# Norm sums by output groups, a first chunk in row quarters, and one split moved, in a two-layer MLA / RG-LRU / MoE trunk

## What is computed

```python
DEPTH = 2; D_MODEL = 1024; T = 16 meta tokens + 256 tokens = 272
for l in range(DEPTH):
    u = rmsnorm(h, norm_mix_g[l])                  # norm 1
    cq, ckv, kr, xr, gt = split(u @ w_in[l])       # 384, 256, 32, 512, 512 columns
    att = mla_mixer(cq, ckv, kr, ...)              # 8 heads, QK-norm, rotary keys
    rnn = rglru_mixer(xr, gt, ...)                 # conv, gates, linear recurrence, gelu gate
    h = h + concat(rmsnorm(att), rmsnorm(rnn)) @ w_out[l]
    u = rmsnorm(h, norm_ffn_g[l])                  # norm 2
    h = h + (swiglu(u), 2816 wide | moe_swiglu(u), top 2 of 8 experts, 1408 wide)[l]
return h[:, N_META:]
```

## Time and profile before

| | us |
|---|---|
| median of three runs | 901.33 |
| the profiled execution | 902.6 |
| its span | 900.6 |
| TensorE busy in it | 868.4 (96%) |
| VectorE busy | 683.5 (76%) |
| ScalarE busy | 574.1 (64%) |
| chain that ended last, on TensorE | 81% |

### The profile page before, as it was taken

One profiled execution on the slowest core, in us unless ns is written; L12 is line 12 of the kernel. 1 busy time (PEld: TensorE's weight loads), 2 busy tenths in 40 slices (PEclk: granted clock), 3 DMA queues, 4 the chain that ended last, 5 costly groups with the idle time before them and its releaser, 6 DMA issues.

```text
span 900.6 us, 15424 instructions
## 1 busy us (share of the span) xinstructions
PE 868.4 (96%) x5825; PEld 798.1 (89%) x5825; DVE 683.5 (76%) x919; ACT 574.1 (64%) x787; POOL 69.5 (8%) x92
## 2 busy tenths in 40 slices
PE   5998999999999999999999999999999999999995
PEld 4965799999999999966899989999998989999994
DVE  5777877666666554787877889799897989789892
ACT  6476656455544443476746777877778777777772
POOL 4450010000000000000132000000000000000000
PEclk9999999999999999999999999999999999999998
DMA  9614025455478553414054899899998999899991
GB/s 299 202 48 142 2 95 187 142 186 179 160 208 236 150 170 112 141 48 140 8 211 170 295 355 373 307 350 400 338 396 300 375 370 364 315 361 380 356 350 27
DMA packets 120748, 208.18 MB, mean 231 GB/s; under 512 B 5872, under 2 KB 73712, under 8 KB 120688
## 3 DMA queue, kind: packets, MB, share of 16 engines
q1 hardware_dynamic: 118976, 201.94, 63.7%
q0 software_dynamic: 1424, 5.24, 2.9%
q10 hardware_dynamic: 288, 0.20, 0.1%
HBM read 202.12 MB, written 5.24 MB: 230 GB/s over the span
## 4 chain that ended last, share of the span: by engine, by line
PE 81%; DVE 10%; ACT 4%; issue 2%; POOL 2%; DMA 1%; SPq 0%; DVEq 0%; ACTq 0%; POOLq 0%
PE ps L2427 24%; PE ps L2452 13%; PE ps L637 11%; PE ps L639 11%; PE ps L638 11%; DVE wlo L1382 4%; PE ps L2392 2%; PE ps L2157 2%; PE ps L1964 1%; ACT whi L940 1%; PE ps L2207 1%; DMA raw<-in_w_in_dram 1%; PE ps L2041 1%; PE ps L2439 1%; PE ps L1969 1%
## 5 line engine op out<-in xcount | busy, mean ns | idle before, releaser
L1382 DVE TENSOR_TENSOR wlo<-raw,whi 128x1536 fp32r<-128x1536 f32 (+4 forms) x296 | 437.9, 1502 | 97.2 <-ACT whi L940 94.6
L940 ACT ACTIVATE whi<-raw 128x1536 fp32r<-128x1536 f32 (+4 forms) x296 | 375.8, 1283 | 159.9 <-PE ps L639 93.2
L637 PE MATMUL ps<-uhi,whi 128*128 128x272 f32 (+1 forms) x576 | 169.9, 295 | 11.6 <-DVE wlo L1382 10.4
L639 PE MATMUL ps<-uhi,wlo 128*128 128x272 f32 (+1 forms) x576 | 166.9, 290 | 0.0
L638 PE MATMUL ps<-ulo,whi 128*128 128x272 f32 (+1 forms) x576 | 166.4, 289 | 0.0
L2427 PE MATMUL ps<-whi,xeh 128*128 128x320 f32 (+1 forms) x512 | 125.7, 326 | 0.0
L2427 PE MATMUL ps<-wlo,xeh 128*128 128x320 f32 (+1 forms) x512 | 124.3, 324 | 0.0
L2427 PE MATMUL ps<-whi,xel 128*128 128x320 f32 (+1 forms) x512 | 124.3, 324 | 0.0
L637 PEld LDWEIGHTS ps<-uhi,whi 128*128 128x128 f32 (+1 forms) x576 | 108.8, 189 | 13.3 <-issue 11.2
L638 PEld LDWEIGHTS ps<-ulo,whi 128*128 128x128 f32 (+1 forms) x576 | 109.1, 189 | 0.5
L639 PEld LDWEIGHTS ps<-uhi,wlo 128*128 128x128 f32 (+1 forms) x576 | 108.8, 189 | 0.0
(11 more groups left out here) (298 smaller groups left out, 1212.6 us busy)
## 6 DMA issues: line engine op xcount, KB each, us to landing
raw<-in_moe_w_down_dram SPq DMA_DIRECT2D x24, 1536.0 KB, 8.9
raw<-in_moe_w_gate_dram SPq DMA_DIRECT2D x16, 1536.0 KB, 7.3
raw<-in_moe_w_up_dram SPq DMA_DIRECT2D x16, 1536.0 KB, 8.3
raw<-in_moe_w_gate_dram SPq DMA_DIRECT2D x16, 1280.0 KB, 9.3
raw<-in_moe_w_up_dram SPq DMA_DIRECT2D x16, 1280.0 KB, 9.1
raw<-in_ffn_w_gate_dram SPq DMA_DIRECT2D x11, 1024.0 KB, 5.2
raw<-in_ffn_w_up_dram SPq DMA_DIRECT2D x11, 1024.0 KB, 5.1
raw<-in_ffn_w_down_dram SPq DMA_DIRECT2D x8, 1408.0 KB, 6.8
```

The lines of the kernel that those rows point to most:

```text
L637: pe.matmul(dst, wh, xh, start=start, stop=False, skip_group_check=True)
L639: return pe.matmul(dst, wl, xh, start=False, stop=stop, skip_group_check=True)
L940: act.activation(placed(whi, s, src), src, ACT.Copy).then_inc(hi_done, 1)
L1382: dve.tensor_tensor(placed(wlo, s, src), src, placed(whi, s, src).bitcast(F32), ALU.subtract).then_inc(lo_done, 1)
```

## The change

1. `total` over 8 chunks becomes `total_by_groups`: chunk c goes to output partitions 32 (c mod 4) to 32 (c mod 4) + 31, with 32 columns of ones. ScalarE copies the bank to SBUF, and one matmul with 128 columns of ones adds up the 128 partitions (`total`), so that the scale is divided by 32 more. The groups' sum of norm 1 stands behind q2 and the last matmul behind kv0 (both layers); of norm 2 of layer 0, behind dense blocks 0 and 1.
2. The recurrent half's squares likewise: 4 matmuls of 32 columns, a copy to `tb` by VectorE, and one single-column matmul for each tile, one step later in the loop of `values`. On VectorE `averages(2)` moves ahead of `normed(0)` and `normed(1)`.
3. w_in's first chunk is split in four row quarters (two token chunks, all 384 columns), in both layers. The three q blocks are done quarter by quarter in three banks (18 matmuls a quarter). In layer 0 the loads are in quarters too, the tokens' first quarter on ScalarE's queue, and the constants and positions behind the second chunk of w_in. MIX_SPLIT becomes 23.
4. Pieces kv0, kv1 and kr are split before the root, and the others five blocks ahead by number.
5. Five fp32 matmuls on a constant tile at the start of TensorE's list (WARM).
6. In w_out, `out_turned(0)`, `out_turned(1)` and `scale_spread` move behind block 1, and `out_turned(2)` behind block 2.
7. The fourth dense piece (`ff(3)`) is split behind the last chunk of `hT` and no longer ahead of it.

```diff
-MIX_SPLIT = 22
+PARTS = 4
+MIX_SPLIT = 23
+WARM = 5
...
+            def later(k):
+                return [PARTS + 3] if k == 0 else [k + SPL + 1] if k >= QC else []
...
+                        for m in range(PARTS):
+                            v = slice(2 * m, 2 * m + 2)
+                            if m:
+                                sp.dma_start(hT[:, v, :], ins["tokens"][:, v, :]).then_inc(x_in[m], 16)
+                            sp.dma_start(slot_of(n, k, c)[:, v, :], src[:, v, :]) ...
...
+                    if not l and j == 1:
+                        sp.dma_start(con[:, :], ins["constants"]).then_inc(con_in, 16)
+                        sp.dma_start(posi[:, :], positions.to_broadcast([P, SEQ])).then_inc(pos_in, 16)
...
+            act.dma_start(hT[:, 0:2, :], ins["tokens"][:, 0:2, :]).then_inc(x_in[0], 16)
             act.dma_start(vec[:, :], ins["columns"]).then_inc(vec_in, 16)
-            act.dma_start(posi[:, :], positions.to_broadcast([P, SEQ])).then_inc(pos_in, 16)
...
+            for m in range(PARTS):
+                first_high(2 * m)
+                first_high(2 * m + 1)
+                mix(0, m)
+            first_squares(range(KD))
+            mix(0, PARTS, PARTS + 1, PARTS + 2)
...
-                    mix(l, 2, 3)
-                root_all(B[l, "n1ss"], rsb[:, :], D, n1_root)
+                    mix(l, 2, 3, PARTS, PARTS + 1, PARTS + 2)
+                take(B[l, "n1part"], rsb[:, :])
+                root_all(B[l, "n1ss"], rsb[:, :], ROPE * D, n1_root)
...
-                    mix(l, k + SPL)
+                    mix(l, *later(k))
...
-                    if m >= SPL and l == 0:
+                    if m >= SPL and l == 0 and m < KD - 1:
                         ff(m - SPL)
...
                 if l == 0:
+                    ff(KD - 1 - SPL)
                     mark(ACT.Sqrt)
                     act.wait_ge(n2_filled, 1)
+                    act.activation(rsb[:, :], ps[:, 4, 0:T], ACT.Copy).then_inc(n2_part, 1)
+                    act.wait_ge(n2_filled, 2)
...
+                group_sums()
+                turned(2, META)
+                rn_variance()
                 mix(l, N_IN + 2)
-                rn_variance()
-                turned(2, META)
+                averages(2)
                 if l == 0:
                     normed(0)
                 normed(1)
-                averages(2)
...
+            def total_by_groups(bk, src):
+                for c in range(KD):
+                    g = c % 4
+                    q = pe.matmul(ps[ROPE * g:ROPE * (g + 1), bk, 0:T], ones(slice(0, P), ROPE), src[:, c, :],
+                                  start=(c < 4), stop=(c >= 4), skip_group_check=True)
                 return q
+            def total(bk):
+                return pe.matmul(ps[:, bk, 0:T], ones(slice(0, P), P), rsb[:, :], start=True, stop=True)
...
+            for _ in range(WARM):
+                pe.matmul(ps[:, 7, 0:T], rr[:, 0:P], rr[:, :], start=True, stop=True)
...
+                def query_latents():
+                    for part in range(PARTS):
+                        s = SPLIT0[l] + part
+                        chunk_ready(s)
+                        for c in range(QC):
+                            b = B[l, "q", c]
+                            if part == 0:
+                                fill(pe, b)
+                            for k in range(2):
+                                kk = 2 * part + k
+                                if c == 0:
+                                    pe.wait_ge(ulo_done, 2 * KD * l + kk + 1)
+                                ...
+                                q = matmul3(pe, bank(b), w, normed_in(kk, slice(0, T)), kk == 0, kk == KD - 1)
...
+                def squares_by_groups():
+                    for c in range(CH):
+                        q = pe.matmul(ps[ROPE * c:ROPE * (c + 1), b.bank, c0:T], ones(slice(0, P), ROPE), ta[:, c, c0:T],
+                                      start=True, stop=True, skip_group_check=True)
...
-                        for c in range(CH):
-                            q = pe.matmul(ps[0:n, b.bank, t:t + 1], ta[:, c, lead:lead + n], one[:, :], start=(c == 0),
-                                          stop=(c == CH - 1))
+                        q = pe.matmul(ps[0:n, b.bank, t:t + 1], tb[:, 0, lead:lead + n], one[:, :], start=True, stop=True)
...
-                    if m == 0:
+                    if m == 1:
                         if l == 0:
                             out_turned(0)
                         out_turned(1)
                         scale_spread()
-                    if m == 1:
+                    if m == 2:
                         out_turned(2)
```

More of the change, by code:

```diff
@@ L461, in build @@
         emptied = [sem(f"emptied{b}") for b in range(8)]
-        x_in = [sem(f"x{n}_in") for n in range(2)]
-        first_in = [sem(f"first{n}_in") for n in range(2)]
+        x_in = [sem(f"x{n}_in") for n in range(PARTS)]
+        first_in = [sem(f"first{n}_in") for n in range(PARTS - 1)]
+        part_used = sem("part_used")
         con_in = sem("con_in")
@@ L929, in split @@
             def split(s, land, src, i=0, chunks=0):
-                if land == MIX0[0] and s < QC - 1:
+                if land == MIX0[0] and s < PARTS - 1:
                     act.wait_ge(first_in[s], 16)
@@ L938, in split @@
                 elif s >= SPL:
-                    act.wait_ge(filled, piece_used(s - SPL) + 2 * chunks * i)
+                    old = [(l, s - SPL - SPLIT0[l]) for l in range(DEPTH) if 0 <= s - SPL - SPLIT0[l] < PARTS - 1]
+                    if old:
+                        act.wait_ge(part_used, (PARTS - 1) * old[0][0] + old[0][1] + 1)
+                    else:
+                        act.wait_ge(filled, piece_used(s - SPL) + 2 * chunks * i)
                 act.activation(placed(whi, s, src), src, ACT.Copy).then_inc(hi_done, 1)
@@ L1701, in _ @@
                         mix(l, N_IN + SPL + m)
-                    elif l == 0:
+                    elif l == 0 and m < KD - 1:
                         ff(m - SPL)
@@ L1959, in sums @@
                 return q
-            def total(bk, src, n):
-                for c in range(n):
-                    q = pe.matmul(ps[:, bk, 0:T], ones(slice(0, P), P), src[:, c, :], start=(c == 0), stop=(c == n - 1))
-                return q
+            def total_by_groups(bk, src):
[3 more added lines that the diff above has]
+                                  start=(c < 4), stop=(c >= 4), skip_group_check=True)
+                return q
+            def total(bk):
+                return pe.matmul(ps[:, bk, 0:T], ones(slice(0, P), P), rsb[:, :], start=True, stop=True)
             def spread(bk, row, width=P):
@@ L2135, in gate_half @@
                         fill(pe, b)
-                    q = dense_block(b, SPLIT0[l] + k, ks, W_IN_PIECES[k][2], 0, normed_in, start=half == 0, stop=half == 1)
+                    q = dense_block(b, SPLIT0[l] + PARTS - QC + k, ks, W_IN_PIECES[k][2], 0, normed_in, start=half == 0, stop=half == 1)
                     if half:
@@ L2179, in values @@
                         if t == 2 and i == VAR_AT:
+                            squares_by_groups()
+                        if t == 2 and i == VAR_AT + 1:
                             variance()
@@ L2307, in group @@
                                 pe.wait_ge(nsq_done, 2 * KD)
-                                total(4, u32, KD).then_inc(n2_filled, 1)
+                                total_by_groups(4, u32).then_inc(n2_filled, 1)
+                            if not per and m == 1:
+                                pe.wait_ge(n2_part, 1)
+                                total(4).then_inc(n2_filled, 1)
                     group([0, 1, 2, 3], FFS0, 0, 0, [B["ff0", q].before for q in range(4)])
```

118 lines of the change are left out of this document (62 added, 56 removed).

## The result

The changed kernel takes 897.65 us (median of 20 runs, 894.47 to 901.96) where the kernel before takes 902.38 (20 runs, 900.82 to 907.41): a ratio of 0.9941, interval 0.9928 to 0.9953. By the ratio that is 5.3 us less (4.2 to 6.5), by the two medians alone 4.7. The forecast was 7.1 us less. The two profiled executions differ by more, 902.6 and 894.47 us (spans 900.6 and 892.5, 8.1 apart).

What follows compares the result with a forecast made beforehand. TensorE, busy 96% of the span, was taken as the bound; 4.5 (start) + 0.2 (layer 1's norm 1) + 2.4 (norm 2) + 0 (output projection) = 7.1 us off 901.33 gives 894.2, own range 892 to 897, 8 in 10 889.5 to 898.5.

Steps and rivals of the forecast that it cites:

- The start: Layer 0 to the latents' sum: first matmul at 8.6 us, TensorE waits 1.5 us at that sum, 4.5 us won.
- rival 2: Start: warm-ups end too soon or do not count, first 20 matmuls at 0.226, 2.1 us more, 896.3; chance 0.20.
- I take it as up: Start: TensorE's clock is already up after 4.6 us of warm-up matmuls, so matmuls take 0.125 us each.
- The norms: Layer 1's norm 1 wins 0.2 us; layer 0's norm 2 wins 2.4, 0.6 of it by the moved split.
- The drains of 0.3 us: Grouped sums: tiling-mode changes might drain TensorE twice each; at 0.3 us, three norms would lose 1.8, time 896.
- The recurrent squares and the transposes: Output projection, both layers: about 0.6 us won by grouping, spent in a 1 us wait at `mixlo`; 0 in all.
- What is left of 6.1 us is 4.6: Layer 0: kv1 begins 6.1 us sooner, a 1.5 us wait follows at the latents' sum, the rest reaches the end.
- the existing fall: TensorE's clock granted at 0.69 and 0.63 between 85 and 95 us; vanishing would widen the range by 2 to 3.
- Rival 3: Clock falls at four new TensorE waits, at most 3.0 us each; four give 906.2, slower than before; chance 0.04.
- last sign of being wrong: Anywhere in the kernel: the forecast is wrong if the clock falls in other places.

Runs made afterwards that it cites:

- e9: The changed kernel with the loads of the constants and positions ahead of the second weight chunk again: 896.81 us, ratio 0.9932.
- e10: The kernel of e7 with the loads of the constants and positions ahead of the second weight chunk: 891.93 us, ratio 0.9900.
- a0: The changed kernel itself run again, unedited, for a second profile: 899.5 us, ratio 0.9947.
- e1: The changed kernel without the five warm-up matmuls: 896.32 us, ratio 0.9935.
- e4: The changed kernel with ScalarE's squares of the latents taken as soon as their own blocks are scaled: 896.02 us, ratio 0.9929.
- e3: The changed kernel with the three norms' squares summed by eight full matmuls instead of four groups, single matmul kept: 904.25 us, ratio 1.0015.
- e8: The changed kernel with the split of the fourth dense piece ahead of the last low part again: 898.45 us, ratio 0.9952.
- e2: The changed kernel with the transposes of the attention's output back at their old places: 896.09 us, ratio 0.9935.
- e5: The changed kernel with the latents' root, xr0's convolution and the reciprocal ahead of the split of the first gate piece: 896.89 us, ratio 0.9932.
- b0: The kernel before the change run again, unedited, for a second profile: 902.41 us, ratio 0.9991.
- e6: The changed kernel with e4's and e5's orders together, and VectorE's convolution of xr1 behind its scaling of the latents: 891.62 us, ratio 0.9890.
- e7: The kernel of e6 with the transposes at their old places as in e2: 890.70 us, ratio 0.9869.

## Why the prediction was right, and where it was off

**The number.** 897.65 us lies inside the range of 8 in 10 (889.5 to 898.5), but 0.65 outside the forecast's own 892 to 897, and 3.4 above the 894.2 predicted. Of that, 1.05 is the starting point: the sum was taken off a median of three runs (901.33), and twenty runs of the same kernel gave 902.38. The other 2.4 is the gain: 4.7 by medians where 7.1 was forecast.

**The start: right in time, luckier than argued.** Forecast 4.5 us at the latents' sum, measured 4.39; the first matmul at 8.04, not 8.6. TensorE's wait there was to be 1.5 us and is 2.31: TensorE ended xr0 0.5 us sooner than in the sum (31.03), and VectorE's chain from the reciprocal to the scaled kr, begun 0.6 sooner, took 8.9 us and not 8.2, because three of its splits were 0.1 to 0.3 us longer each, beside POOL's work on the angles. The earlier start paid for that. The Trainium skill, GPSIMD Engine Reference, 1. Specifications, says that GpSimd shares its SBUF interface with VectorE, with contention where a VectorE instruction has two SBUF inputs; the trace agrees: the splits (raw and whi) stretch, while the scalings, which read one operand from PSUM, stay at 0.44. In e9, where POOL's work ends 4.9 us sooner (29.3 us), all three splits take 1.22; but not every split beside POOL is longer (the one at 31.81 took 1.23), and in e10 two of the three stretch again. So this cause is likely, and not shown.

**The warm-ups: rival 2 is a matter of the execution.** Of eleven profiled executions with warm-ups, nine start at full pace and two (a0, e9) run at 0.226 to about 12.0 us, although the warm-ups lie at 2.57 to 7.47 us in both a0 and the first profile. The price is 1.8 us at the grouped sum (19.01 and 17.25), where rival 2 had 2.1. Without them (e1) the grouped sum comes at 18.45, so in these single executions warm-ups that work win 1.2 us and warm-ups that fail lose 0.6. The prediction's "I take it as up" was right in nine of eleven, with less margin than it seemed: in the nine, the first clock record of the trace, a rise to full, lies between 5.88 and 8.04 us, in one of them (e4) only as the first product begins.

**The norms: right.** Norm 2 and layer 1's norm 1 were to win 2.6 and won 2.61 (layer 1's own stage, from q0's first matmul to the latents' sum, 24.55 and 24.78 before: 0.2, as forecast); a grouped sum has the 1.15 us that the earlier trace rows gave, e3 puts 2.5 on each, e8 0.54 on the moved split. The drains of 0.3 us that the prediction weighed against it do not show: from the grouped sum's first matmul to the next block it is 1.06 us (17.25 to 18.31), and the steps into it and behind it (17.04 to 17.25, 18.31 to 18.54) are each 0.1 us longer than the pace.

**The recurrent squares and the transposes: right.** Forecast 0 with a wait of 1 us at `mixlo`; measured waits 0.97 and 1.06, stages -0.10 and -0.27. e2 shows both halves.

**The step that failed: "What is left of 6.1 us is 4.6", passed on to the end.** I followed VectorE as far as the latents' sum, in both layers, and let everything behind it come earlier by the same amount. In layer 1 it did not: 1.22 us were lost between that sum and the scores, and 0.18 in layer 0, where another loss was won back (there the kernel before waited 0.82 us for VectorE in the head norms' stage, and that wait is gone):

```profile
70.62 1.55 PE L2101 MATMUL ps<-raw,ckv 128*128 128x512 f32 x3 [0.82 <-DVE ksq L1491]
```

The cause, shown by e5: the whole chain ran closer to the transfer of the first gate chunk. That transfer is issued when VectorE has split the chunk whose buffer it takes, and lands at 34.6:

```profile
28.07 1.33 DVE L1400 TENSOR_TENSOR wlo<-raw,whi 128x1024 fp32r<-128x1024 f32 x1
...
29.43 0.37 SPq L704 DMA_DIRECT2D raw<-in_w_in_dram  x1
```

ScalarE and VectorE reach its split first; VectorE stands still for 2.25 us, and the reciprocal and the scalings for the query blocks stand behind that split in its queue. e5 takes them out from behind it, and the wait of 1.06 us and the loss in layer 1 are gone. The two losses, 1.22 and 0.18, are 1.40 of the 2.15. The rest is small: 0.11 at the start, 0.10 and 0.27 in the stages of the projections (forecast 0), and 0.28 behind layer 1's `mx`, whose cause stays open.

**The clock: the existing fall counted on neither side.** Rival 3 asked whether the new waits bring falls. Behind the wait at the latents' sum, or behind e4's in its stead, four of nine profiles have one (e2, e4, e8, a0), 1.1 to 1.3 us each at the scores and next to nothing in e4; of the five profiles without such a wait (before, b0, e6, e7, e10) none has. That speaks for the mechanism, at a price well under the 3.0 that I gave it and only in some executions; four in nine against none in five is too few to call it shown. By the prediction's last sign of being wrong, a fall in another place, a0 is a miss: 35.85 us is such a place. Over many runs it costs nothing that can be seen: the mean granted clock was 0.9909 in 20 runs of the changed kernel and 0.9894 in a0's nine, 0.9897 and 0.9902 in 22 and 8 runs of the kernel before. So the falls that the new waits may bring are no more than those that come anyway, and no part of the measured difference can be put down to rival 3.

## What to carry to other kernels

Follow a won stretch past the wait that ends it: walk the queue of the engine that is now late to its next instruction on the path, and ask which of the instructions between waits for a transfer or a buffer that nobody hurried. Taking away the largest wait wins nothing while another chain is as late (e4: 0; e5: 1.7; both with one more order, e6: 4.0, all by stages): order by who waits for the result. Compare two spans by stages before you compare their ends, for a fall of the clock in one of them can be as large as the change.

## What the runs showed of the hardware beyond that

- The view of the granted clock says nothing of the start. a0's matmuls between 8 and 12 us come every 0.226 us, and the clock of that stretch reads 1.00. The first clock record of that trace is a rise at 11.96 us, and the view counts what lies ahead of it as full; the first record is at 10.89 in e1, 11.94 in e9 and 15.18 in the kernel before, each where the pace rises:

```profile
8.00:12.00 4.00, 3.97 (x17) 3.98 (x18) 4.00 (x8) 4.00 (x9) 0.03 (x1) 1.00 1.07 387
```

- The slow stretch had 3.0 us of work (e1), 4.0 (a0), 4.7 and 5.2 (b0) in four executions, and warm-ups of 4.9 us followed by 0.55 us without work gave both outcomes.
- One program's spans differed by 7.7 us with all its stages outside the clock's falls within 0.2 us.
- A full fp32 sum of eight matmuls costs 3.7 us, four column groups 1.1 for the same eight, with steps in and out of 0.21 and 0.23 us where the pace is 0.125.
